# GpSimd takes the probability scaling, the weight low halves and the query low half of the second attention

## What is computed

```
c_q, c_kv, k_rope = split(h @ w_a, [384, 640]);  c_q, c_kv = rms_norm(...) * gains
q  = (c_q @ w_uq)  -> 16 heads of 64 + 32 (the 32 rotated by position)
kv = (c_kv @ w_ukv) -> 16 heads of 64 (keys) + 64 (values); the rotated key part is shared
p  = softmax(causal((q_nope . k_nope + q_rope . k_rope) * (64 + 32) ** -0.5))
o  = p @ v;   y = o @ w_o
```

## Time and profile before

| | us |
|---|---|
| median of 3 runs | 1498.39 (1496.3 to 1501.65) |
| the profiled execution, its own time | 1497.74 |
| its span in the trace | 1496.0 |
| the second attention's heads, in the trace | about 863 to 1045 |
| clock granted to TensorE, mean | 0.962 of full speed |

### The profile page before, as it was taken

The page is one execution under the profiler, slowest core; times in us unless marked ns, Lnnn a source line. Parts: engine busy times, 40 slices in busy tenths (PEclk is TensorE's granted clock), DMA queues, the critical chain, the costliest instruction groups (busy, mean ns, idle before and its releaser), DMA issues.

```text
span 1496.0 us, 19764 instructions
## 1 busy us (share of the span) xinstructions
PE 1379.3 (92%) x6615; PEld 1056.9 (71%) x6615; DVE 837.0 (56%) x1400; ACT 584.4 (39%) x1040; POOL 10.0 (1%) x20
## 2 busy tenths in 40 slices
PE   5799999989799999999997788888879999999997
PEld 2567777756566767888884566666757888888885
DVE  2645565644655555664335668888456666665333
ACT  4434444432423232332223356666334444432222
POOL 2000000000000000000000000000000000000000
PEclk8799999979899999999998899999989999999998
DMA  9522112108376665333332111112113333333321
GB/s 349 164 87 57 43 56 56 43 1 266 104 248 241 230 234 169 98 94 94 93 100 56 33 32 28 30 26 65 57 56 90 94 97 98 98 98 90 103 90 69
DMA packets 224292, 154.67 MB, mean 103 GB/s; under 512 B 28637, under 2 KB 214450, under 8 KB 220146
## 3 DMA queue, kind: packets, MB, share of 16 engines
q1 hardware_dynamic: 224242, 154.01, 33.0%
HBM read 151.89 MB, written 2.10 MB: 103 GB/s over the span
## 4 chain that ended last, share of the span: by engine, by line
PE 79%; DVE 8%; ACT 5%; issue 5%; DMA 2%; SPq 1%; ACTq 0%; DVEq 0%
PE pj L1251 65%; PE sc L1401 3%; PE ov L1439 2%; PE tr L1421 2%; DVE nmax L961 2%; PE sc L1302 2%; ACT wh L514 1%; PE sc L1406 1%; DMA first_ada<-in_ada_w_dram 1%; DMA ada_w_sb<-in_ada_w_dram 1%; PE ov L1293 1%; DVE tmp L1170 1%; PE sc L1308 1%; ACT tmp L598 1%; DVE wl L836 1%
## 5 line engine op out<-in xcount | busy, mean ns | idle before, releaser
L836 DVE TENSOR_TENSOR wl<-raw,wh 128x1024 fp32r<-128x1024 f32 (+2 forms) x215 | 235.6, 1096 | 401.2 <-ACT wh L514 400.5
L1251 PE MATMUL pj<-hh,wh 128*128 128x512 f32 x1000 | 409.2, 409 | 41.1 <-DVE wl L836 10.1
L514 ACT ACTIVATE wh<-raw 128x1024 fp32r<-128x1024 f32 (+2 forms) x215 | 205.3, 955 | 534.0 <-PE pj L1251 528.6
L1251 PE MATMUL pj<-hl,wh 128*128 128x512 f32 x1000 | 394.9, 395 | 0.0
L1251 PE MATMUL pj<-hh,wl 128*128 128x512 f32 x1000 | 394.8, 395 | 0.0
L1251 PEld LDWEIGHTS pj<-hh,wh 128*128 128x128 f32 x1000 | 190.3, 190 | 112.9 <-issue 37.6
L1251 PEld LDWEIGHTS pj<-hh,wl 128*128 128x128 f32 x1000 | 190.6, 191 | 41.3
L1251 PEld LDWEIGHTS pj<-hl,wh 128*128 128x128 f32 x1000 | 191.3, 191 | 34.8 <-issue 0.2
L1251 PE MATMUL pj<-gh,wh 128*128 128x512 f32 x512 | 204.1, 399 | 7.7 <-DVE gl L982 5.1
L1251 PE MATMUL pj<-gl,wh 128*128 128x512 f32 x512 | 201.2, 393 | 0.0
L1251 PE MATMUL pj<-gh,wl 128*128 128x512 f32 x512 | 200.9, 392 | 0.0
(11 more groups left out here) (163 smaller groups left out, 1343.8 us busy)
## 6 DMA issues: line engine op xcount, KB each, us to landing
raw<-in_ffn_w_in_dram SPq DMA_DIRECT2D x88, 512.0 KB, 3.8
ada_w_sb<-in_ada_w_dram SPq DMA_DIRECT2D x36, 1024.0 KB, 6.1
raw<-in_ffn_w_out_dram SPq DMA_DIRECT2D x32, 448.0 KB, 3.4
raw<-in_fox_w_in_dram SPq DMA_DIRECT2D x24, 512.0 KB, 3.8
first_ada<-in_ada_w_dram SPq DMA_DIRECT2D x8, 1024.0 KB, 9.5
raw<-in_ffn_w_out_dram SPq DMA_DIRECT2D x16, 512.0 KB, 3.6
first_ada<-in_ada_w_dram SPq DMA_DIRECT2D x1, 4096.0 KB, 24.7
raw<-in_fox_w_o_dram SPq DMA_DIRECT2D x8, 512.0 KB, 5.7
```

Of the source, the lines that this page charges most:

```text
L514: act.activation(wh[:, n0 % 2, 0:kt, :], raw[:, n0 % 2, 0:kt, :], ACT.Copy).then_inc(w_hi, 1)
L836: dve.tensor_tensor(wl[:, n0 % 2, 0:kt, :], raw[:, n0 % 2, 0:kt, :], f32(wh[:, n0 % 2, 0:kt, :]), ALU.subtract).then_inc(w_lo, 1)
L1251: ins = pe.matmul(bank_[:, :], (wl if term == 2 else wh)[:, s, kt, :], (rl if term == 1 else rh)(kt), start=start and j == 0, stop=stop an ...
```

## The change

Three kinds of work of the second attention go from VectorE to GpSimd: the scaling of the probabilities, the subtraction that makes `wl` for the chunks from the head loop on (those of the first four head chunks stay, and the output projection's first two go along), and the query's low half. GpSimd gets a program of its own, with the same steps, written out for all eight trips. VectorE keeps the reciprocal (`inverse`). The query's scale factor moves forward into `mla_nope` (ScalarE) and `mla_rotate` (VectorE, now a scalar_tensor_tensor), so that ScalarE's query copy has none and the low half is a plain subtraction of two SBUF operands. `ev_d` counts the query's tile at `mla_rotate` and no longer at the low half; the low half has a semaphore of its own, `q_lo`, for which the scores of b = 0 wait.

```diff
@@ -307,7 +307,7 @@
         o_hi = sem("o_hi")
         o_lo = sem("o_lo")
         nope = sem("nope")
-        rot = sem("rot")
+        q_lo = sem("q_lo")
         kr = sem("kr")
         k_hi = sem("k_hi")
         kr_hi = sem("kr_hi")
@@ -501,6 +501,48 @@
                                    base=-32 * part, pattern=[[-1, HEADS], [0, P]], channel_multiplier=1
                                    ).then_inc(pc, 1)
 
+            def weight_low(n0, i, per, nxt):
+
+                n = nxt + n0 if nxt is not None else i * per + n0
+                kt = chunk_k(nxt + n0 if nxt is not None else n0)
+                pool.wait_ge(w_hi, n + 1)
+                pool.wait_ge(w_lo, n)
+                pool.tensor_tensor(wl[:, n0 % 2, 0:kt, :], raw[:, n0 % 2, 0:kt, :],
+                                   wh[:, n0 % 2, 0:kt, :].bitcast(F32), ALU.subtract).then_inc(w_lo, 1)
+
+            def normalise(u, unit):
+
+                nc_ = (u % QB + 1) * P
+                c = slice(u % 8, u % 8 + 1)
+                pool.wait_ge(rinv_s, unit + 1)
+                pool.tensor_scalar(prob[u % 4][:, 0:nc_], prob[u % 4][:, 0:nc_], rinv[:, c], None,
+                                   ALU.mult).then_inc(pn, 1)
+
+            def query_low(h, par, tile_q):
+                pool.wait_ge(ev_a, tile_q + 1)
+                pool.tensor_tensor(q_tile(gl, par), mq, q_tile(gh, par).bitcast(F32), ALU.subtract).then_inc(q_lo, 1)
+
+            query_low(0, 0, T_MLA)
+
+            def mla_step(t, s, fill, nxt):
+                j, b = s // QB, s % QB
+                n0 = C_MLA + 2 * (j + 1)
+                t0 = t * 4 + (T_MLA + 2 * (j + 1))
+                if s <= 8 and (s or not first(t)):
+                    normalise(s - 1, t * 8 + (U_MLA + s - 1))
+                if fill and b == 1:
+                    weight_low(n0 + 2, t, 4, nxt)
+                if fill and b == 2:
+                    query_low(t * 2 + (j + 1), 1 - j, t0)
+                    weight_low(n0 + 3, t, 4, nxt)
+
+            last = HEADS // 2 - 1
+            for t in range(last):
+                for s in range(8):
+                    mla_step(t, s, True, None)
+            for s in range(12):
+                mla_step(last, s, s < QB, 4 * last)
+
 
         @block.scalar
         def _(act):
@@ -760,13 +802,13 @@
 
             def mla_nope(n_q):
                 act.wait_ge(mm, n_q + 1)
-                act.activation(mq[0:HD, :], PJ[T_MLA % 2][0:HD, :], ACT.Copy).then_inc(nope, 1)
-
-            def mla_take(h, par):
+                act.activation(mq[0:HD, :], PJ[T_MLA % 2][0:HD, :], ACT.Copy, scale=MLA_SCALE).then_inc(nope, 1)
+
+            def mla_take(h, par, tile_q):
 
                 act.wait_ge(nope, h + 1)
-                act.wait_ge(rot, h + 1)
-                act.activation(q_tile(gh, par), mq, ACT.Copy, scale=MLA_SCALE).then_inc(ev_a, 1)
+                act.wait_ge(ev_d, tile_q + 1)
+                act.activation(q_tile(gh, par), mq, ACT.Copy).then_inc(ev_a, 1)
 
             def mla_take_kv(par, n_kv):
                 act.wait_ge(mm, n_kv + 1)
@@ -775,7 +817,7 @@
 
             split_after(C_MLA, 0, 0, 0)
             mla_nope(C_MLA)
-            mla_take(0, 0)
+            mla_take(0, 0, T_MLA)
             split_after(C_MLA + 1, 0, 0, 0)
             mla_take_kv(0, C_MLA + 1)
 
@@ -801,7 +843,7 @@
                     split_after(n0, t, 4, nxt)
                     mla_nope(t * 4 + n0)
                 if fill and b == 2:
-                    mla_take(t * 2 + (j + 1), 1 - j)
+                    mla_take(t * 2 + (j + 1), 1 - j, t * 4 + (T_MLA + 2 * (j + 1)))
                     split_after(n0 + 1, t, 4, nxt)
                     mla_take_kv(1 - j, t * 4 + (n0 + 1))
 
@@ -961,12 +1003,17 @@
                 dve.tensor_reduce(nmax[:, u % 8:u % 8 + 1], SC[u % 2][:, 0:nc_], AX.X, ALU.max, negate=True
                                   ).then_inc(nmax_s, 1)
 
-            def normalise(u, unit):
-
-                nc_ = (u % QB + 1) * P
+            def inverse(u, unit):
+
                 c = slice(u % 8, u % 8 + 1)
                 dve.wait_ge(expd, unit + 1)
                 dve.reciprocal(rinv[:, c], rsum[:, c]).then_inc(rinv_s, 1)
+
+            def normalise(u, unit):
+
+                nc_ = (u % QB + 1) * P
+                c = slice(u % 8, u % 8 + 1)
+                inverse(u, unit)
                 dve.wait_ge(rinv_s, unit + 1)
                 dve.tensor_scalar(prob[u % 4][:, 0:nc_], prob[u % 4][:, 0:nc_], rinv[:, c], None,
                                   ALU.mult).then_inc(pn, 1)
@@ -1167,14 +1214,8 @@
             def mla_rotate(h, n_q):
                 dve.wait_ge(mm, n_q + 1)
 
-                dve.tensor_tensor(mq[HD:P, :], PJ[T_MLA % 2][HD:P, :], rope_sb[HD:P, :], ALU.mult
-                                  ).then_inc(rot, 1)
-
-            def mla_take(par, tile_q):
-                dve.wait_ge(ev_a, tile_q + 1)
-                dve.scalar_tensor_tensor(out=q_tile(gl, par), in0=mq, scalar=MLA_SCALE,
-                                         in1=f32(q_tile(gh, par)), op0=ALU.mult, op1=ALU.subtract
-                                         ).then_inc(ev_d, 1)
+                dve.scalar_tensor_tensor(out=mq[HD:P, :], in0=PJ[T_MLA % 2][HD:P, :], scalar=MLA_SCALE,
+                                         in1=rope_sb[HD:P, :], op0=ALU.mult, op1=ALU.mult).then_inc(ev_d, 1)
 
             def mla_take_kv(h, par, tile_kv):
                 dve.wait_ge(ev_a, tile_kv + 1)
@@ -1184,7 +1225,6 @@
 
             split_after(C_MLA, 0, 0, 0)
             mla_rotate(0, C_MLA)
-            mla_take(0, T_MLA)
             split_after(C_MLA + 1, 0, 0, 0)
             mla_take_kv(0, 0, T_MLA + 1)
 
@@ -1196,7 +1236,7 @@
                 if s < 8:
                     maximum(s, t * 8 + (U_MLA + s))
                 if s <= 8 and (s or not first(t)):
-                    normalise(s - 1, t * 8 + (U_MLA + s - 1))
+                    inverse(s - 1, t * 8 + (U_MLA + s - 1))
                 if s < 8 and b == 3:
                     dve.wait_ge(tr_hi, R + (MLA_TR * j + 2))
                     dve.tensor_tensor(v_half(gl, j), tr_half((R_MLA + MLA_TR * j + 1) % 2),
@@ -1209,11 +1249,8 @@
                 if b == 3 and h is not None:
                     o_take(h % 2, t + h // 2, t * 2 + (H_MLA + h))
                 if fill and b == 1:
-                    split_after(n0, t, 4, nxt)
                     mla_rotate(t * 2 + (j + 1), t * 4 + n0)
                 if fill and b == 2:
-                    mla_take(1 - j, t0)
-                    split_after(n0 + 1, t, 4, nxt)
                     mla_take_kv(t * 2 + (j + 1), 1 - j, t0 + 1)
 
             for s in range(8):
@@ -1225,6 +1262,7 @@
             for s in range(12):
                 mla_step(last, s, s < QB, 4 * last)
             dve.wait_ge(gate_ok, 3)
+            dve.wait_ge(w_lo, C_MLAO + 2)
             dense(C_MLAO, T_MLAO, 2, 5)
             norm(5)
             modulated(3, 5)
@@ -1613,6 +1651,7 @@
                 if s < 8:
                     if b == 0:
                         pe.wait_ge(ev_d, t0)
+                        pe.wait_ge(q_lo, t * 2 + (j + 1))
                     scores(s, t * 8 + (U_MLA + s), slice(0, P), j, b)
                 v = turned_unit(t, s)
                 if v is not None and v < 8:
```

More of the change, by code:

```diff
@@ L962, in maximum @@
                                   ).then_inc(nmax_s, 1)
+            def inverse(u, unit):
+                c = slice(u % 8, u % 8 + 1)
+                dve.wait_ge(expd, unit + 1)
+                dve.reciprocal(rinv[:, c], rsum[:, c]).then_inc(rinv_s, 1)
             def normalise(u, unit):
@@ L967, in normalise @@
                 c = slice(u % 8, u % 8 + 1)
-                dve.wait_ge(expd, unit + 1)
-                dve.reciprocal(rinv[:, c], rsum[:, c]).then_inc(rinv_s, 1)
+                inverse(u, unit)
                 dve.wait_ge(rinv_s, unit + 1)
```

## The result

The changed kernel takes 1520.26 us (median of 4 runs, 1518.37 to 1525.87), the kernel before 1498.59 over the runs made beside them. The ratio is 1.0157, 95% interval 1.0131 to 1.0183: slower by 1.6%. The forecast was 1489.4, faster, with a range that ended at 1498.

A forecast was written before the change was run, and what follows sets the result against it. A head's length was taken to come from a loop of waits across engines. Per head 0.74 - 0.22 = 0.52 us, over 15 intervals, plus 1.20 gives 9.0: 1498.39 - 9.0 = 1489.4 us, range 1485 to 1498.

The forecast's parts named there:

- term s: GpSimd's work time for the 512-element scaling between reciprocal and transposes, taken as 0.63 us; gain 15 x (1.15 - s) + 1.2.
- GpSimd's scaling becomes the loop: Rival: the 512-element scaling between reciprocal and transposes makes the kernel slower, 1505.4 us at 1.7, 1510.0 at 2.00; chance 0.13.
- the loop loses 0.74 us: Query chunk's weight low half leaves VectorE, so the rotation directly follows the turned low half: 0.74 us gained per head.
- lost at the next wait: Rival: the earlier maximum finds TensorE or ScalarE unready for what follows; 0 to 3 us gain, about 1497; chance 0.05.
- The 1.20 of the last head: Last head's 1024-element weight low half moves to GpSimd, taking 1.94 - 0.74 = 1.20 us more away.
- the query low half and the key/value chunk's low half: On VectorE both sit between two waits for ScalarE; taking them away gives no gain.
- the two-input lengths on GpSimd: Subtractions of two SBUF inputs: about 1.09 us for 512 elements, 0.64 for 256, 0.86 for 384.
- the query's earlier bank release and the `q_lo` wait: TensorE's step-0 fill could start 0.7 us earlier but gains zero; `q_lo` is passed before the key wait.
- the rotation directly behind the turned low half: Sign of being right: on VectorE the rotation starts 0.03 us behind the turned low half.
- The 384 scaling: Step-2 scaling on GpSimd at 0.52 us: TensorE could transpose at 959.62, does so at 959.66 now; no cost.
- a 512 scaling of 1 us or more: Sign of being wrong: GpSimd's 512-element scaling at 1 us or more, where 0.6 to 0.8 was expected.
- transposes waiting for GpSimd: Sign of being wrong: TensorE's transposes wait for GpSimd in steps 0 and 2 and not in step 1 alone.

The follow-up runs named there:

- step 3 alone: Changed kernel with only step 3's 512-element scaling on GpSimd, other scalings back on VectorE, both subtractions still on GpSimd: 1512.17 us, ratio 1.0083.
- the two-tensor form: Changed kernel with GpSimd's scaling written as tensor_tensor with a repeated factor column instead of tensor_scalar: 1508.63 us, ratio 1.0076.
- values-first pair: TensorE turns new values before multiplying the previous head's probabilities: on the changed kernel with scaling on VectorE 1486.05 us; on the kernel before 1498.78 us.
- the subtractions alone: Changed kernel with the probability scaling back on VectorE, weight and query low halves still on GpSimd: 1498.01 us, ratio 0.9989.
- the order alone: Kernel before the change, with only TensorE turning the new head's values before multiplying the previous head's probabilities: 1498.78 us, ratio 1.0006.
- the wait filled: Changed kernel with five more 512-column matmuls before the scores of step 0, their result overwritten: 1510.88 us, ratio 1.0093.
- step 2 alone with the wait filled: Changed kernel with only step 2's 384-element scaling on GpSimd, others on VectorE, plus five throwaway matmuls before step 0's scores: 1504.11 us, ratio 1.0034.
- the step-2 kernel: Changed kernel with only step 2's 384-element scaling on GpSimd, other scalings on VectorE, both subtractions on GpSimd: 1523.96 us, ratio 1.0173.

## Why the prediction was wrong

It asked for a head of 11.12 us (11.64 - 0.52) and got 13.60, 2.48 us off. The runs split that into three:
- **The scaling's length, 0.93 us.** The term s of the sum was taken as 0.63 from the `affine_select` row and measured 1.56. The point from which the sum turns to a loss was put at 1.23, so this step alone decides the sign. Its way of counting was sound: reciprocal, 0.15, s, 0.13, transposes. Beside the 11.62 of the kernel with the scaling on VectorE it gives 11.62 + s - 0.405, so 12.78 for step 3 alone (measured 12.74) and 12.26 for the two-tensor form (12.21). The rival "GpSimd's scaling becomes the loop" had this mechanism and 13%, with 1505.4 at s = 1.7.
- **The relief, 0.73 us.** "It lies in the loop ... the loop loses 0.74 us. Is the cover there?" was answered by ScalarE's 1.32 us of idle time before the exponential. The step that failed is that check: it looked at the first instruction released and not at the next ones. The values' copy starts at 955.06 before the change, and its other input, the value transposes, is done at 954.99:

```profile
954.53 0.46 PE L1627 MATMUL tr<-ident,tmp 64*128 64x64 f32 x4
...
955.06 0.38 ACT L795 ACTIVATE gh<-tr 128x256 fp32r<-128x256 f32 x1
```

Seven hundredths of a microsecond separate the end of the one path from the start of the copy, and the copy needs some of them: with the scaling on VectorE it started 0.04 behind the transposes that it waited for (954.89 and 954.93). So the loop had two nearly equal branches and the change cut one. The rival "lost at the next wait" said so and got 5%, on the ground of idle time that was not in the branch that mattered. The values-first pair shows it: 0.01 us a head from the subtractions alone (11.63 to 11.62), nothing from the order alone (11.63), 0.74 with both (10.90). So the forecast's 0.74 was short by 0.73. The 1.20 of the last head failed and came back the same way: 12.69 to 12.95 with the subtractions alone, and 12.68 to 10.75, 1.93 of the 0.74 + 1.20, with the order changed.

- **The clock, 0.86 us.** 13.60 against 12.74 with the wait filled. No part of the prediction priced it. The steady stretch read 1.00, and the waits of 0.86 and 0.66 us brought nothing. That the wait before the step-2 transposes would grow from 0.66 to 1.30, and what the clock would do then, was not asked.

These come to 2.52, 0.04 more than the gap they explain.

What was right: the query low half and the key/value chunk's low half on VectorE cost nothing (moving them changed no steady head); the two-input lengths on GpSimd within 0.2 us up to 512 elements (1024 were put at 2.0 and took 2.36); the query's earlier bank release and the `q_lo` wait without effect; the rotation directly behind the turned low half. The 384 scaling was said to cost nothing, with 0.04 us of slack, at 0.52 us of work; at 1.24 it costs 0.4 us a head (step 2 alone with the wait filled, 12.02 - 11.62) and brings the slow stretch. That 0.4 does not add to the 512 scaling's cost: with all scalings on GpSimd and the wait filled the head is 12.74, as with step 3 alone. Of the signs named for a wrong outcome, "a 512 scaling of 1 us or more" and "transposes waiting for GpSimd" appeared.

## What to carry to other kernels

Before counting an instruction taken out of a loop as gain, follow the released chain instruction by instruction and note for each the end of its other inputs: the smallest of those gaps bounds the gain, and here it was 0.07 us of 0.74, of which 0.01 came. An operation moved to GpSimd is priced by a run of that very instruction, not by a neighbour of the same shape; of two forms of the same product one took half as long again (1.56 and 1.04 us). Such a probe has to run clear of VectorE instructions with two SBUF inputs, or its times mix two causes. And a new wait of TensorE is to be priced with the clock that follows it, which filling the wait with throwaway matmuls tests in one run.

## What the runs showed of the hardware

- On GpSimd, float32, 128 partitions: `tensor_scalar` 0.60, 0.92, 1.24 and 1.56 us for 128 to 512 elements (2.5 ns an element); the product with a repeated column by `tensor_tensor` 0.40, 0.61, 0.83 and 1.04 (1.7 ns); a subtraction of two tensors in the kernel 0.73, 1.01, 1.29 and 2.36 for 256, 384, 512 and 1024. At the program's start, beside VectorE's additions with two SBUF inputs, the two-tensor product took 0.85 and 1.15 us for 128 and 384 elements.
- Behind waits of 0.58 and 1.30 us, with four short matmuls between, TensorE was at 1.2 GHz for some 3.5 us in each steady head of after, and in 11 of 14 heads of the step-2 kernel. Behind 0.29 and 1.38 us, in the first full head of after, it was not. Behind 0.58 and 0.86 it was in one head of 14 (the two-tensor form), and behind 0.56 and 0.67 in no steady head (scaling on VectorE).
- VectorE's 256-element subtraction with two SBUF inputs took 1.31 us beside a GpSimd subtraction, and 0.42 alone; those with one input in PSUM did not get longer. Its 256-element scaling, SBUF to SBUF, took 1.75 us once, beside a 1024-element subtraction on GpSimd of 2.39 us, and 0.35 in the other heads; it ended 0.15 us after GpSimd's instruction.
